# Two neighbouring 2 MB gate-up transfers of an expert step become one transfer of 4 MB

## The reference

```python
for e in range(N_EXPERTS):                      # 8 experts
    out = out + gates[:, e:e + 1] * _swiglu(hf, w_gate[e], w_up[e], w_down[e])

def _swiglu(h, w_gate, w_up, w_down):           # 1024 -> 3584 -> 1024
    return (jax.nn.silu(h @ w_gate) * (h @ w_up)) @ w_down
```

## Time and profile before

| | |
|---|---|
| median of 3 runs | 1518.24 us (1517.54 to 1518.34) |
| the profiled execution, its own time | 1516.15 us |
| its span, first to last instruction | 1514.3 us |
| PE busy | 1429.0 us (94%) |
| DMA packets | 44202, 493.91 MB, mean 326 GB/s |
| transfers of the expert weights | 136 into `ring`, 32 into `arena`, 2048 KB each |

### The profile page before, as it was taken

One profiled execution on the slowest core, in us unless ns is written; L12 is line 12 of the kernel. 1 busy time (PEld: TensorE's weight loads), 2 busy tenths in 40 slices (PEclk: granted clock), 3 DMA queues, 4 the chain that ended last, 5 costly groups with the idle time before them and its releaser, 6 DMA issues.

```text
span 1514.3 us, 44722 instructions
## 1 busy us (share of the span) xinstructions
PE 1429.0 (94%) x19890; PEld 1078.4 (71%) x19890; DVE 372.2 (25%) x1021; ACT 159.0 (11%) x378; POOL 138.2 (9%) x230
## 2 busy tenths in 40 slices
PE   4998999999999898899999999989989989999996
PEld 3886788888887787666667767757757766765554
DVE  2814240212112714211111111111111111113334
ACT  2102120010012203100000000000000000000001
POOL 0000040330400000000000000000000000000000
PEclk8998999999999999999999999999999999999999
DMA  9946587656517903949999999999999999999870
GB/s 385 422 163 261 212 334 278 246 188 233 195 56 289 397 11 156 384 180 385 426 427 410 426 427 413 426 426 408 428 426 422 421 425 419 416 425 402 353 316 29
DMA packets 44202, 493.91 MB, mean 326 GB/s; under 512 B 4896, under 2 KB 5152, under 8 KB 5792
## 3 DMA queue, kind: packets, MB, share of 16 engines
q1 hardware_dynamic: 41040, 475.02, 76.4%
q10 hardware_dynamic: 3024, 16.73, 2.7%
HBM read 478.10 MB, written 13.63 MB: 325 GB/s over the span
## 4 chain that ended last, share of the span: by engine, by line
PE 81%; DMA 12%; DVE 4%; ACT 1%; issue 1%; SPq 0%; POOL 0%; POOLq 0%; DVEq 0%
PE PS L743 30%; PE PS L443 20%; PE PS L752 15%; DMA ring<-in_expert_stream 8%; PE PS L597 5%; DMA arena<-in_expert_stream 2%; PE PS L427 2%; DMA ring<-in_dense_stream 2%; PE PS L761 2%; PE PS L723 1%; DVE arena L1051 1%; PE PS L651 1%; PE PS L567 1%; PE PS L579 1%; PE PS L475 1%; PE PS L417 1%
## 5 line engine op out<-in xcount | busy, mean ns | idle before, releaser
L743 PE MATMUL PS<-ring,arena 128*32 128x256 f32 x7040 | 403.3, 379 | 24.0 <-DMA ring<-in_expert_stream 15.4
L743 PEld LDWEIGHTS PS<-ring,arena 128*32 128x32 f32 x7040 | 256.8, 110 | 150.0 <-issue 18.4
L443 PE MATMUL PS<-arena,ring 128*128 128x256 f32 x1408 | 311.3, 381 | 4.2 <-ACT arena L854 2.7
L443 PEld LDWEIGHTS PS<-arena,ring 128*128 128x128 f32 x1408 | 267.2, 191 | 44.1 <-issue 6.0
L752 PE MATMUL PS<-ring,arena 128*32 128x256 f32 x4928 | 297.0, 379 | 0.8 <-DVE consts L1051 0.8
L752 PEld LDWEIGHTS PS<-ring,arena 128*32 128x32 f32 x4928 | 183.4, 110 | 83.6 <-issue 1.4
L743 PE MATMUL PS<-arena 128*32 128x256 f32 x2816 | 163.1, 382 | 7.8 <-DMA arena<-in_expert_stream 5.4
L1051 DVE TENSOR_TENSOR stat<-stat,PS 128x128 f32<-128x128 f32 x154 | 44.2, 287 | 502.5 <-ACT stat L1009 502.5
L1051 DVE TENSOR_TENSOR arena<-arena,PS 128x256 f32 (+1 forms) x123 | 55.2, 449 | 372.7 <-PE PS L443 234.5
L743 PEld LDWEIGHTS PS<-arena 128*32 128x32 f32 x2816 | 106.6, 111 | 55.8 <-issue 6.8
L1601 POOL COPY arena<-arena 128x256 f32 x153 | 61.3, 401 | 812.9 <-PE PS L743 764.3
(11 more groups left out here) (187 smaller groups left out, 603.9 us busy)
## 6 DMA issues: line engine op xcount, KB each, us to landing
ring<-in_expert_stream SPq DMA_DIRECT2D x136, 2048.0 KB, 19.6
ring<-in_dense_stream SPq DMA_DIRECT2D x105, 1024.0 KB, 7.7
arena<-in_expert_stream SPq DMA_DIRECT2D x32, 2048.0 KB, 22.8
ssm_scratch<-arena ACTq DMA_DIRECT2D x12, 1024.0 KB, 5.0
ring<-ssm_scratch SPq DMA_DIRECT2D x12, 1024.0 KB, 9.8
arena<-in_xt ACTq DMA_DIRECT2D x1, 1024.0 KB, 13.8
arena<-in_ssm_small ACTq DMA_DIRECT2D x1, 1024.0 KB, 9.2
out_t<-arena ACTq DMA_DIRECT2D x4, 256.0 KB, 2.5
```

The lines of the kernel that those rows point to most:

```text
L443: mm = pe.matmul(PS[:, bank, j * T:(j + 1) * T], w[:, c, j * P:(j + 1) * P], moving[:, c, :], start=(c == 0), stop=(c == NC - 1))
L743: mm = pe.matmul(PS[32 * q:32 * q + 32, 0, 0:256], hbuf[:, c * BLK:(c + 1) * BLK], w[:, q * 256:(q + 1) * 256], start=(c == 0), stop=(c == ...
```

## The change

The layout of the expert weights in HBM is changed on the host for the pairs that are joined, so that each partition's two rows of 16 KB lie behind one another. `joined_pairs` lists the first numbers of the gate-up pairs whose slots are neighbours within one buffer. By the plan these are 55 of the 56 steps: all but step 2, whose transfers 6 and 7 sit in slots 6 and 0. For a joined pair SP waits for both slots, as before in the order of the numbers, and issues nothing at the first number and one transfer of 4 MB (128 rows of 32 KB) at the second. Both halves then count as loaded by one semaphore, that of the first slot. The matmuls are the same.

```diff
+def joined_pairs():
+
+    firsts = range(0, ROUNDS * EXPERTS * STEP, STEP)
+    return [n for n in firsts if PAIR_PLAN[n + 1][0] == PAIR_PLAN[n][0] + 1 != RING // 2]
+
+
 PAIR_PLAN = pair_plan()
+JOINED = joined_pairs()
...
-        def pair_slot(n):
+        def pair_slot(n, pairs=1):
             s = PAIR_PLAN[n][0]
             if s < RING // 2:
-                return ring[:, 2 * s * PIECE:(2 * s + 2) * PIECE]
+                return ring[:, 2 * s * PIECE:2 * (s + pairs) * PIECE]
             s -= RING // 2
-            return more[:, 2 * s * PIECE:(2 * s + 2) * PIECE]
+            return more[:, 2 * s * PIECE:2 * (s + pairs) * PIECE]
...
         def pair_full(n):
 
+            n = n - 1 if n - 1 in JOINED else n
             s = PAIR_PLAN[n][0]
             dense_uses = sum(m % RING == 2 * s for m in range(PRE)) if s < RING // 2 else 0
-            return pair_sem(n), 16 * (dense_uses + sum(PAIR_PLAN[m][0] == s for m in range(n + 1)))
+            return pair_sem(n), 16 * (dense_uses + sum(PAIR_PLAN[m][0] == s and m - 1 not in JOINED for m in range(n + 1)))
...
             def load_pair(n):
-                sp.dma_start(pair_slot(n), expert_in[n]).then_inc(pair_sem(n), 16)
+                if n - 1 in JOINED:
+                    first = pair_slot(n - 1, 2)
+                    both = expert_in[n - 1:n + 1].rearrange("k p w -> (k p w)").rearrange("(p w) -> p w", p=P)
+                    sp.dma_start(first, both).then_inc(pair_sem(n - 1), 16)
+                elif n not in JOINED:
+                    sp.dma_start(pair_slot(n), expert_in[n]).then_inc(pair_sem(n), 16)
...
+    for n in JOINED:
+        expert_stream[n:n + 2] = expert_stream[n:n + 2].transpose(1, 0, 2).reshape(2, P, 2 * PIECE)
```

## The result

The changed kernel takes 1530.93 us (median of 4 runs, 1529.47 to 1534.52) against 1518.29 us of the kernel before (1517.54 to 1521.56): ratio 1.0085, 95% interval 1.0064 to 1.0106. It is 12.6 us slower. Forecast was 1521.8 us, with a range up to 1526.5: the direction was right, the size three to four times too small.

The account below looks back on a forecast made before the run. The prediction took DMA to bound rounds 1 to 5 and PE the last; -2.2 us for longer rows, +4.9 for round 0 and +0.9 for step 49 gave +3.6 on 1518.2, so 1521.8 us, range 1515.5 to 1526.5.

Parts of the forecast that it names:

- What bounds the kernel: Rounds 1 to 5 go at the DMA engines' pace, PE close behind; from step 49 PE decides to the end.
- Term 1: Joined pairs between transfers 12 and 148: fewer, longer rows save 0.047 us a pair, 2.2 us gained (0 to 9.2).
- the sign: From 692 to 750 us, a DMA rate of 427 to 428 GB/s would show the gain from longer rows.
- (d): Each row of 32 KB is moved as two of 16, so almost no gain: +5.8, 1524.0 us; chance 0.07.
- (e): Rows of 32 KB run slower, 4.5 us lost in place of the gain: +10.3, 1528.5 us; chance 0.06.
- Term 2: In round 0 transfer 12 waits for 13's slot, so its work leaves an idle DMA gap: 4.9 us lost.
- Term 3: PE waits for the whole pair before a first product: hidden in rounds 1 to 5, 0.9 us lost at step 49.
- cover: In rounds 1 to 5 the queue absorbs later issues: transfers 60 and 61 are issued 4.6 us before 59 lands.
- (c): PE's clock falls behind longer waits, covered in rounds 1 to 5 but not at step 49: +5.2, 1523.4 us; chance 0.10.
- The sum: Over the whole kernel, -2.2 + 4.9 + 0.9 = +3.6 us, giving 1521.8 us, 0.24% slower.

Follow-up runs that it names:

- join_late_spin: The changed kernel with pairs joined only from step 8 on and unused matmuls ahead of PE's wait in expert 1's steps; ratio 1.0008 against the kernel before.
- hold_round0: The kernel before, with SP holding transfers 9, 12, 15, 18 and 21 of round 0 until their neighbours' slots are free, none joined; 1525.06 us, ratio 1.0040.
- wait_both_last: The kernel before, with PE waiting for both gate-up transfers only in the last round's steps, no transfer changed; ratio 1.0027.
- wait_both: The kernel before, with PE waiting for both gate-up transfers ahead of a step's first product, no transfer changed; 1529.43 us, ratio 1.0068.
- join_from_round1: The changed kernel with pairs joined only from step 8 on, round 0 as before; 1527.16 us, ratio 1.0050 against the kernel before.
- join_16k_rows: The changed kernel with rows of 16 KB, two per partition, in its 4 MB transfers, weights in HBM laid out as before; ratio 1.0104 against the kernel before.
- before_spin: The kernel before, with three unused matmuls between the halves of the first product of expert 1's steps from round 1 on; ratio 1.0001.
- changed_again: The changed kernel itself measured once more, as a mark for other runs; ratio 1.0093 against the kernel before.
- wait_both_spin: The kernel before, with PE waiting for both gate-up transfers and unused matmuls ahead of that wait in expert 1's steps; ratio 1.0020.

## Why the prediction was wrong

**What bounds the kernel: right.** The DMA engines set rounds 1 to 5, and PE the last one. But "with PE close behind" was as far as it went, and the two are coupled both ways: PE's products release the slots.

**Term 1, right and small.** A full stretch of before, then the same 40 us of the changed kernel (columns as in rows 3):

```profile
840.00:880.00 40.00, 39.18 (x729) 28.27 (x724) 7.15 (x23) 1.94 (x7) 2.81 (x7) 1.00 1.01 426
```

```profile
840.00:880.00 40.00, 39.31 (x732) 24.98 (x728) 7.15 (x23) 1.94 (x7) 2.81 (x7) 1.00 1.00 428
```

426 against 428 GB/s: by the landings, the 3 x 4.89 = 14.7 us of a step become 9.73 + 4.89 = 14.6, or 0.06 us a pair where 0.047 was taken. (From 692 to 750 us the changed kernel shows 430 GB/s, where the prediction had named 427 to 428 as the sign.) Rows of 32 KB are neither cut in two nor slower, so rivals (d) and (e) fall. The Trainium skill's rates for rows a large power of two apart ("DMA: Bandwidth & Descriptors", section "Latency and other measured facts") have no counterpart here at 32 KB. Nor does the 2.0 us of fixed time that the Trainium skill has for each DMA (same page, section "Anatomy of one DMA", a fit for transfers issued from GpSimd, where these are SP's): 48 transfers fewer in join_late_spin are worth nothing that 1.0008 (0.9992 to 1.0023) can show. No run shows that the 2 us of term 1 reach the end of the kernel.

**Term 2, right.** Predicted 4.9 us; alone it measured 6.1 (3.6 to 8.5) in hold_round0, and 5.0 us at step 9 of its trace. (Its lower value is 4.9 - 1.1 = 3.8 us, not 3.7.)

**Term 3 is the step that failed.** It said that in rounds 1 to 5 the wait for the whole pair is hidden: by the wait for the down weights behind it, and by "cover" in the queue if it were not. The first half holds only at full clock. The arithmetic that let the product end at 1012.4, the very time of the next landing, left no margin at all, and the clock fall adds 2.8 us to the product (from its start to that of the down product 6.25 us, where it is 3.45 at full clock). The second half was misread. The issue of transfer 60 lies 4.6 us ahead of the landing of 59, but an issue needs time until its data moves: transfer 13, issued to a queue that had just run empty, took 7.8 us where a transfer behind others adds 4.9, so of those 4.6 us at most 1.7 were cover. Its own landing stands in the trace of before:

```profile
L375 SPq DMA_DIRECT2D arena<-in_expert_stream x1: 328/328/328, 916.9 to 916.9; - x1
DMA to landing us min/median/max: 10.2/10.2/10.2
```

Transfer 60 landed at 927.1, 5.6 us behind transfer 59 and not 4.9. In wait_both_last the same transfer with the same lead landed 4.9 behind, so 4.6 us is about where the queue begins to run dry; with leads of 1.8 to 2.9 us, as in wait_both, 1.0 to 2.5 us are lost each time. Where the prediction had 0.9 us for the wait for both, and all of it in step 49, wait_both measured 10.3.

**Rival (c) had the mechanism and the wrong places.** It named the clock and gave it a chance of 0.10, because the trace of before had one fall in five rounds, behind 2.77 us, and none behind 2.37 (nor behind 2.85 at 1127 us, which it did not name). But the change makes each of these waits 1.7 us longer, to about 4 us, and for that length the trace of before had no row. In the four traces of the changed kernel (two), wait_both and join_from_round1, a fall stands behind 17 of the 18 waits of 3.9 us or more; join_16k_rows has five more such waits and five falls. And rival (c) priced the fall at step 49 only, since it took over the wrong cover. The 10.3 us (6.4 to 14.1) of wait_both are what term 3 and (c) should have been together.

The Trainium skill has this case: "TensorE: Matmul & The Clock Gate", section "HAM oscillation — how this bites in real kernels", describes a kernel in which each wait for a DMA lets the clock fall, so that every tile behind a wait starts slow. The traces agree for waits of 3.9 us and more, with 6.43 us for 3.66; shorter ones went either way. To be held against the change ahead of time, it had to be asked how long each wait of PE would be after it, and not only how much waiting there is in total.

**The sum, done again from the runs.** Term 2 alone 6.1 us, the wait for both alone 10.3, and a gain of about 2 at most make 14 to 16 where 12.6 were measured, within the intervals.

## What to carry to other kernels

Before a wait is made coarser, list how long the engine will stand still in each place afterwards, and ask what its clock does there and who waits for what it releases; a wait that seems hidden by the next one is hidden only as long as the work between them keeps its speed. Here half a product done ahead of the wait was enough to make a clock fall harmless. The lead of an issue is no cover by itself: compare the distance of the two landings with that in a full queue. And joining neighbours is free only where both slots come free together, which the first turn of a ring may not do although every later one does.

## What the runs showed of the hardware

TensorE's granted clock fell behind waits as short as 2.04 us (before_spin), and 1.94 in the last 15 us of the changed kernel, and it stayed up behind others of 3.06 (join_from_round1) and 3.15 (wait_both_last), so for waits of 2 to 3 us it can't be told from the wait alone; behind 3.9 us and more it fell in 17 of 18 (the one it stayed up behind was 3.92, in changed_again). With 2.7 us of unused matmuls in such a wait (2.3 in the last round) it stayed up in every expert step from round 1 on of join_late_spin and wait_both_spin. A transfer of 4 MB with a lead of 2.3 us landed 11.2 us behind the one before it, against 9.7 in a full queue, and one of 2 MB with a lead of 2.2 us (transfer 84 in wait_both) 6.7 against 4.9. And transfers of 4 MB in rows of 32 KB, with 2 MB ones between, moved at 428 GB/s over 40 us of full queue, where 2 MB ones in rows of 16 KB alone reach 426.
